# A decoder step with paged caches: cached keys rearranged ahead of the kernel and loaded page by page, and more expert columns folded on VectorE

## The reference

```python
def compressed_branch(q, pos, kv, w1, b1, w2):
    ...
    sub = kv.reshape(bsz, kv.shape[1] // CMP_STRIDE, CMP_STRIDE, 2, A_KV, A_DH)
    first = jnp.einsum('bnlcgd,cldh->bncgh', sub, w1[:, :CMP_STRIDE])
    second = jnp.einsum('bnlcgd,cldh->bncgh', sub, w1[:, CMP_STRIDE:])
    hid = jax.nn.gelu((first[:, :-1] + second[:, 1:]).astype(jnp.float32) + b1.astype(jnp.float32)[:, None, :], approximate=False)
    ckv = jnp.einsum('bncgh,chd->bncgd', hid.astype(kv.dtype), w2)
    ...
```

## Time and profile before

| | |
|---|---|
| median of 3 runs | 2576.49 us (2570.51 to 2578.44) |
| profiled execution, its own time | 2571.7 us |
| its span | 2569.9 us |
| mean granted clock of TensorE | 0.861 of 2.4 GHz |
| busy: TensorE, VectorE, ScalarE, GpSimd | 1970.7, 1468.7, 916.4, 942.9 us |
| moved by DMA | 805.61 MB, mean 313 GB/s |

### The profile page before, as it was taken

The page is one execution under the profiler, slowest core; times in us unless marked ns, Lnnn a source line. Parts: engine busy times, 40 slices in busy tenths (PEclk is TensorE's granted clock), DMA queues, the critical chain, the costliest instruction groups (busy, mean ns, idle before and its releaser), DMA issues. The chain is left out here.

```text
span 2569.9 us, 23064 instructions
## 1 busy us (share of the span) xinstructions
PE 1970.7 (77%) x6950; PEld 981.6 (38%) x6950; DVE 1468.7 (57%) x3134; ACT 916.4 (36%) x2462; POOL 942.9 (37%) x839
## 2 busy tenths in 40 slices
PE   5999797788888777977768688875677777739765
PEld 4436565344444334545212345362122333313211
DVE  1025256895666535774874455758447666664564
ACT  1112103687777323631232234412134444422222
POOL 2021033677554323342653332426233333122551
PEclk9975799899899888998889777987789899969979
DMA  6232518978999989898989986976789888989697
GB/s 194 99 143 74 172 54 334 367 320 345 420 420 420 413 332 388 348 405 302 411 347 387 351 328 229 368 292 270 309 339 358 346 346 347 353 291 359 244 420 296
DMA packets 170226, 805.61 MB, mean 313 GB/s; under 512 B 32564, under 2 KB 37176, under 8 KB 86648
## 3 DMA queue, kind: packets, MB, share of 16 engines
q0 software_dynamic: 93552, 673.78, 66.0%
q1 hardware_dynamic: 76408, 130.37, 14.2%
q10 hardware_dynamic: 144, 0.00, 0.0%
HBM read 798.37 MB, written 14.04 MB: 316 GB/s over the span
## 5 line engine op out<-in xcount | busy, mean ns | idle before, releaser
L3076 POOL DMA_INDIRECT g_uv<-in_peer_uv_dram,f_idx x320 | 389.6, 1217 | 642.0 <-PE g_acc L3193 512.3
L3193 PE MATMUL g_acc<-g_uv,g_diag 128*128 128x512 f32 (+1 forms) x848 | 451.7, 670 | 110.8 <-ACT g_diag L3165 109.1
L3119 DVE CUSTOM_DVE_ANT_0 g_uv<-g_uv,f_h 128x1024 f32<-128x1024 f32 x320 | 405.2, 1271 | 212.1 <-DMA g_uv<-in_peer_uv_dram,f_idx 204.4
L3076 POOL DMA_INDIRECT f_u<-in_peer_uv_dram,f_idx x256 | 299.6, 1170 | 491.9 <-PE g_acc L3193 383.9
L3119 DVE CUSTOM_DVE_ANT_0 f_u<-f_u,f_h 128x1024 f32<-128x1024 f32 x256 | 325.0, 1276 | 180.6 <-DMA f_u<-in_peer_uv_dram,f_idx 174.9
L3193 PE MATMUL g_acc<-f_u,g_diag 128*128 128x512 f32 (+1 forms) x676 | 356.4, 661 | 69.3 <-ACT g_diag L3165 51.7
L3145 ACT ACTIVATE g_gelu<-g_dot 128x2 f32<-128x2 f32 x288 | 58.3, 203 | 763.6 <-DVE g_dot L3119 762.4
L3193 PEld LDWEIGHTS g_acc<-g_uv,g_diag 128*128 128x128 f32 (+1 forms) x848 | 156.9, 197 | 353.3 <-issue 336.4
L3193 PEld LDWEIGHTS g_acc<-f_u,g_diag 128*128 128x128 f32 (+1 forms) x676 | 125.4, 198 | 254.8 <-issue 234.1
L1241 PE MATMUL g_side<-g_slab 128*128 128x512 f32 (+3 forms) x288 | 128.9, 589 | 55.0 <-DMA g_slab<-in_nsa_w_in_dram 52.4
L1101 PE MATMUL g_side<-g_slab 128*128 128x512 f32 x256 | 135.9, 613 | 13.6 <-ACT g_slab L1139 11.9
(11 more groups left out here) (406 smaller groups left out, 2678.8 us busy)
## 6 DMA issues: line engine op xcount, KB each, us to landing
g_slab<-in_nsa_w_in_dram SPq DMA_DIRECT2D x15, 2048.0 KB, 19.1
g_slab<-in_peer_w_q_dram SPq DMA_DIRECT2D x14, 2048.0 KB, 22.2
mp_w<-in_mlstm_w_in_dram SPq DMA_DIRECT2D x6, 2048.0 KB, 10.0
g_slab<-in_nsa_w_out_dram SPq DMA_DIRECT2D x6, 2048.0 KB, 8.4
g_slab<-in_state_win_kv_dram SPq DMA_DIRECT2D x8, 1024.0 KB, 7.7
out_win_s_dram<-in_state_win_kv_dram SPq DMA_DIRECT2D x1, 8128.0 KB
g_uv<-in_peer_uv_dram,f_idx POOLq DMA_INDIRECT x320, 10.8
f_u<-in_mlstm_w_out_dram SPq DMA_DIRECT2D x2, 2048.0 KB, 11.0
```

The source lines that it names most:

```text
L3076: pool.indirect_dma_start(both(i), None, table, bass.IndirectOffsetOnAxis(ap=idx[:, col:col + 1], axis=0), element_offset=layer * PK * PK ...
L3119: dve.tensor_tensor_reduce(row(i, 0), row(i, 0), h[:, t, :], 1.0, 0.0, ALU.mult, ALU.add, dot[:, g % DRING, k:k + 1]).then_inc(dotted, 1)
L3193: mm = pe.matmul(acc[0:n, a, :], diag[:, q % DIAGS, 0:n], row(i, 1)[:, a * 512:a * 512 + 512], start=i == opens[s], stop=i == closes[s])
```

## The change

Before the launch the host writes the caches in another order (`turned`): a page's keys with the key's elements across the 128 partitions, as the products read them, and the values as they were. The window and the compressed MLP's weights are rearranged too. In the kernel the transposes (L1090, L2210) and their copies (L1139, L2349, L2351) are gone, and the products read the loaded rows.

GpSimd's 64 gathers of pages (L1075, L2152) are gone. SyncE loads each page by a number that it reads from the page table into a register (`S.page`): 256 loads of 128 KB for the compressed branch (1 KB to a partition, two buffers of 16 pages, a load waits until the products of the unit two before are done) and 128 of 256 KB for the selected one (2 KB to a partition, waiting for the part three before). The compressed branch now runs in 16 units, keys and values of a sequence apart, of 16 beats from beat 32. The MLP's weights come in 3 loads, three times. `load_stage` keeps only the loads. In `SHARES` 42 more columns are folded on VectorE (237 of 512 in place of 195).

```diff
 class Shared:
+    def page(self, sp, b, k):
+        at = NPAGE * b + k
+        return sp.value_load(self.pages[0:1, at:at + 1], min_val=0, max_val=self.I["sel_turned"].shape[0] - 1)
...
 class CachedBlocks:
-    START = 38
-    UNIT = 2 * CSTR
-    TILES = 4
+    START = 32
+    UNIT = 16
+    UNITS = 2 * DEC_B
...
+    def sync(self, sp):
+        S, I = self.S, self.S.I
+        sp.wait_ge(self.first.projected, 2 * NJ)
+        sp.dma_start(self.w1.rearrange("p c k f h -> p (c k f h)"), I["cmp_w1_rows"]).then_inc(self.weights_in, 16)
+        sp.dma_start(self.w2.rearrange("p c d -> p (c d)"), I["cmp_w2_rows"]).then_inc(self.weights_in, 16)
...
+        for b in range(DEC_B):
+            page = [S.page(sp, b, k) for k in range(NPAGE)]
+            for c in range(2):
+                v = 2 * b + c
+                if v >= 2:
+                    sp.wait_ge(self.multiplied, 8 * (v - 1))
+                for k in range(NPAGE):
+                    sp.dma_start(self.rows[:, v % 2, k, :], I["cmp_turned"][bass.ds(page[k], 1), c].rearrange(
+                        "u p n -> (u p) n")).then_inc(self.rows_in[v % 2], 16)
+
+    def product(self, pe, v, k):
+        b, c = divmod(v, 2)
+        if k == 0:
+            pe.wait_ge(self.rows_in[v % 2], 16 * NPAGE * (v // 2 + 1))
...
+        rhs = self.rows[:, v % 2].rearrange("p a (k g n) -> p k g a n", k=8, g=AG)[:, k]
+        pe.matmul(self.ps_h[c].rearrange("p g (a n) -> p g a n", n=8), self.w1[:, c, k].rearrange("p f h -> p (f h)"), rhs,
+                  start=(k == 0), stop=(k == 7)).then_inc(self.multiplied, 1)
...
 class DecodeWork:
-    def turn(self, pe, p, k):
...
+        pe.matmul(self.bank[1][r0:r0 + 32].rearrange("p (l j) -> p l j", l=4), self.q_blk[:, 2 * PARTS[p][1] + b2, a, :],
+                  self.tiles[:, slot, :, 0, a * P:(a + 1) * P], start=True, stop=True).then_inc(self.multiplied, 1)
...
-    def copy_keys(self, engine, e):
...
+        def load(p):
+            branch, u, q = PARTS[p]
+            if p >= 3:
+                sp.wait_ge(self.summed, p - 2)
+            for b2 in range(2):
+                slot = (2 * p + b2) % SLOTS
...
+                for k in range(4):
+                    page = S.page(sp, 2 * u + b2, 4 * q + k)
+                    sp.dma_start(self.rows[:, slot, 2 * GD * k:2 * GD * (k + 1)], I["sel_turned"][bass.ds(page, 1)].rearrange(
+                        "u p n -> (u p) n")).then_inc(self.landed[slot], 16)
...
+        for p in range(3):
+            load(p)
         for u in range(4):
             sp.wait_ge(self.b_done, u + 1)
             save(0, u, self.o_cmp[:, u, :])
...
+        for p in range(3, len(PARTS)):
+            load(p)
+            if p % 4 == 0 and p >= 8:
+                sp.wait_ge(self.o_ready, p // 4 - 1)
+                save(1, p // 4 - 2, self.o[:, p // 4 - 2, :])
...
-SHARES = ((0, (3,)), (160, (1, 3)), (300, (3,)), (393, (1, 3)), (483, ()), (577, (1, 3)), (772, ()), (836, (3,)),
-          (950, (1, 2, 3)), (1154, ()), (1238, (1, 3)))
+SHARES = ((0, (3,)), (160, (1, 3)), (483, (3,)), (577, (1, 3)), (772, (3,)), (836, (1, 3)), (950, (1, 2, 3)),
+          (1154, (3,)), (1238, (1, 3)))
```

More of the change, by code:

```diff
@@ L1063 @@
[L1063 to L1077, removed]
@@ L1081, in turn @@
[L1081 to L1092, removed]
@@ L1094, in product @@
[L1094 to L1102, removed]
+        self.ps_k = S.bank[0][:, 0:2 * P].rearrange("p (a n) -> p a n", a=2)
@@ L1118, in pe @@
         pe.wait_ge(self.weights_in, 16 * self.LOADS)
-        for b in range(DEC_B + 1):
-            for r in range(0, self.UNIT if b < DEC_B else 8, 2):
-                yield from at(self.START + self.UNIT * b + r)
-                q = CSTR * b + r // 2
-                if b < DEC_B:
-                    self.turn(pe, q)
-                if 1 < q <= CSTR * DEC_B + 1:
-                    self.product(pe, q - 2)
-                if r == 6 and b:
-                    self.outputs(pe, b - 1)
-        self.S.leave(pe, self.out_cp, 2 * DEC_B)
@@ L1142, in split @@
-    def split(self, act, b, c):
-        act.wait_ge(self.multiplied, CSTR * b + (14, 16)[c])
-        if b:
-            act.wait_ge(self.pre_ready, 2 * (b - 1) + c + 1)
-        act.activation(self.second[:, c], self.ps_h[c][ADH:P], ACT.Copy).then_inc(self.second_ready, 1)
-    def squash(self, act, b, c):
-        act.wait_ge(self.pre_ready, 2 * b + c + 1)
-        act.activation(self.hid[:, c, :, 0:N_CMP], self.pre[:, c, :, 0:N_CMP], ACT.Gelu, bias=self.b1[:, c:c + 1]
-                       ).then_inc(self.hid_ready, 1)
+        for v in range(self.UNITS + 1):
+            for k in range(8):
+                yield from at(self.START + self.UNIT * v + 2 * k)
+                if v < self.UNITS:
+                    self.product(pe, v, k)
+                if k == 4 and v and v % 2 == 0:
+                    self.outputs(pe, v // 2 - 1)
+                    if v == self.UNITS:
+                        break
@@ L1189, in dve @@
         self.S.enter(dve, 1)
-        for b in range(DEC_B):
-            for c in range(2):
-                yield from at(self.START + self.UNIT * b + 32 + 4 * c)
-                self.meet(dve, b, c)
+        for v in range(self.UNITS):
+            yield from at(self.START + self.UNIT * (v + 1) + 3)
+            self.meet(dve, v)
 NP_JOBS = [(AQW + br * 2 * GD, WB) for br in range(3)] + [(AQW + AKVW, 3 * AH), (0, WB), (WB, WB)]
@@ L1795, in sync @@
             sp.wait_ge(route.scored, NJ)
[L1796 to L1798 removed]
+        proj.sync(sp, t, rows_used)
+        sp.dma_start(self.w2.rearrange("p c d -> p (c d)"), I["cmp_w2_rows"]).then_inc(self.cw_in, 16)
         with S.nc.allow_non_contiguous_dma(reason="128 biases"):
@@ L2145, in pool @@
     def pool(self, pool, at):
-        cached = self.I["cache_sel_kv"][0].rearrange("a (n l) c g d -> (a n) (l c g d)", l=PTOK)
-        def load(p):
-            _, u, q = PARTS[p]
-            for b2 in range(2):
-                slot = (2 * p + b2) % SLOTS
-                pool.indirect_dma_start(self.rows[:, slot, :], None, cached, bass.IndirectOffsetOnAxis(
-                    ap=self.S.quarter_idx[:, q, 2 * u + b2:2 * u + b2 + 1], axis=0)).then_inc(self.landed[slot], 16)
         yield from at(self.beat)
@@ L2942, in __init__ @@
         self.first = FirstRoute(st, S, self.ranks, self.route.keys_in, u_ring, v_ring, more, acc, w_out_in, d_scores)
-        self.cached = CachedBlocks(st, S, self.first, [more[:, 0], more[:, 1]])
+        self.cached = CachedBlocks(st, S, self.first)
         self.vec = st.sem("side_vec")
@@ L3047, in weave_stage @@
         diag_ready, applied, added = (st.sem(n) for n in ("diag_ready", "applied", "added"))
-        work = SideWork(st, Shared(nc, st, M, I, O, h, idx, gate, quarter_idx, added),
+        work = SideWork(st, Shared(nc, st, M, I, O, h, idx, gate, pages, added),
                         u_ring, v_ring, more, acc, w_out_in)
```

266 lines of the change are left out of this document (96 added, 170 removed).

## The result

The median went from 2571.7 us (20 runs) to 2548.7 (19 runs); the ratio is 0.9909, with a 95% interval of 0.9895 to 0.9924. A twentieth run of the changed kernel, at 3447.1 us, was in the slow state and is left out. That is a gain of 23 us where 58 were forecast. The profiled execution took 2542.0 us (span 2540.2), 6.7 under the median of its kind; that of before, 2571.7, was at its median.

What follows compares the result with a forecast made beforehand. The bound changes by stage, in a ring of late TensorE, slots, gathers and dots; −2 − 23 + 22 − 2 − 5 − 8 − 4 − 8 − 5 − 23 = −58 gives 2513.7 profiled, 2518 us median; range 2465 to 2590.

Steps and rivals of the forecast that it cites:

- 1-KB piece: Cached page loads: DMA time of one 1-KB piece, not in the trace, taken as 0.050 us, bounds 0.044 and 0.068.
- The engines stay busy through this; I cost it at nothing: Cached blocks: TensorE stalls on late page units and GpSimd stops, but page loads keep the DMA engines busy; cost 0.
- the −23 of the cached blocks: Cached blocks, 380 to 640 us: without transposes and copies gathers go earlier, DMA share 0.87 to 0.96; −23 us.
- The second rival: Starvation: pages stay late, TensorE stalls, DMA share stays 0.87 in cached blocks and parts; 2573 us, chance 0.16.
- The folds: 42 more columns on VectorE: a quarter of TensorE's freed time in two stages, a third in another; −4, −8, −5 us.
- the −5 before: First prompt work, 850 to 1025 us: weights in one plain load, 12 more folded columns; share already 0.96, so −5 us.
- the +22: Cached blocks: 32768 pieces of 1 KB replace 4096 of 8 KB, 102 us in place of 80; +22 us, bounds +10 and +59.
- TensorE's transposes: 512 go in the cached blocks (79.2 us of TensorE), 320 in the decode parts (53.3 us); −23 us forecast in each stage.
- The parts: Decode parts: transposes, copies and GpSimd's page-gather waits go; transfers need 303 us, 316 at share 0.96; −23 us, bounds 303 or no gain.
- The weights: MLP's weights in plain loads end TensorE's waits of 13.8 and 16.8 us in prompt work; −5 and −8 us.
- SyncE: Page loads move to SyncE: 0.62 us an issue plus 0.5 a register load, 9 us a part against 15; it fits.
- The load stage: Start of the kernel: the product and five VectorE steps that make row numbers go; −2 us.

Runs made afterwards that it cites:

- half units: Changed kernel with the same 256 loads of 128 KB, but units of 8 pages in four buffers of half the size: 2529.35 us, ratio 0.9833.
- both edits: Changed kernel with the decode parts' products two beats earlier and cached pages in 2-KB pieces, one 256-KB load a page: 2512.0 us, ratio 0.9747.

## Why the prediction was too high, point by point

The direction was right and the time lies in the range, even in the forecast's own (2490 to 2555); the size was not, 23 us for 58. That it lies in the narrower range is luck: the width was there for a dearer 1-KB piece, which came out at the price taken. Two steps failed.

- **"The engines stay busy through this; I cost it at nothing".** The paragraph had the mechanism (one for one, a unit late, TensorE stalls, the ring fills) and then let it go free. The engines do stay busy while TensorE waits (1.04), and run dry just after it (0.52), because nothing has been gathered meanwhile. It cost some 19 us: that is what half units took away with the same transfers (a part of the waits is still there), and then the stage stands at 466.1, 1.6 under before, where the forecast without the stall had 3. In the terms of the sum it is the −23 of the cached blocks that was lost: 23 us of idle engines were to go, 8 went (32.7 to 24.3), and with half units 23 (to 9.3). The second rival had this stage at +20 (no fill, dearer pieces), and it came out at +17.5, so this stage went nearly as that rival had it; but its sign, a DMA share of 0.87 in the first half and in the parts, did not show. The share rose to 0.92 and 0.93. A stall of this kind shows in TensorE's waits, and only part of it in the share of the transfers.
- **The folds, −17 in the three stages and a part of the −5 before.** "How much is on the path lies between nothing and all of it"; it was nothing that can be measured, on the kernel before, on the changed one and on the one with both edits. A quarter was a number without a row, and none of the rows shown of before gives it; the run with the old shares does: a stage in which TensorE's busy time differs by 20 us at the same length is not set by TensorE. What sets 368 to 428 stays open. That columns 224 to 272 and 368 to 428 came out at −4.5 and −7.5, as forecast, is luck: the first is hardly more than what profiles of the same code differ by (162.5 to 168.8 in the nine kernels with the new shares, 167.0 before), and the second came with the rest of the change, as the old shares have it too.

The other steps:

- *The 1-KB piece,* taken at 0.050 us: 32768 of them took 49 ns each on the mean, measured over the packets of the trace. The price was right, and with 101 us for the pages where 80 were reckoned before, so was the +22.
- *TensorE's transposes,* worth 23 in the cached blocks and most of the 23 in the parts, with their copies: put back without these they cost 15.8 and 15.7. Mechanism right, the size two thirds; what the copies were worth is not shown.
- *The parts,* −23 forecast, −16.8 measured, at a share of 0.93 in place of 0.96; this is the next largest miss. The products had kept the beats that the transposes had needed; with these moved the stage reached 314.0, where the forecast had 316.
- *The weights,* −13 forecast, 14 by the run with the old loads (6 to 22).
- *SyncE,* 0.5 us for a register load: 0.27 and 0.15 of register work, 1.0 us a page in all where 1.12 were taken. It fits, as forecast.
- *The load stage,* −2: −1.5.

Columns 180 to 224 took 3.6 us longer, which no step foresaw; over all the runs with the change they took 134.5 to 140.7, so this is hardly more than what profiles differ by.

## What to carry to other kernels

Two DMA queues that were both full took turns by pieces here, so a queue of small pieces beside one of large ones got a small part of the bytes: a buffer filled that way needs its lead reckoned at that rate (37 us for 2 MB in 1-KB pieces), and larger pieces, or smaller buffers that are free earlier, gain time though the bytes stay the same. When an argument says that a stall will come, put a price on it, even if the busy share says that nothing is idle. After an operation is taken out, look for the beats, banks and waits that were laid out for it; and before work is moved off an engine, look whether the stage's length follows that engine at all.

## What was not expected of the hardware

The turn between the two queues was exact over 100 us, 4535 packets for 4535, with pieces of 8 KB against 2 KB. And TensorE's granted clock fell where work was taken from it, from 0.88 to 0.80 in the parts, and rose to 0.87 when the transposes were put back, so part of a saving in busy time is given back at the 1.2 GHz level: the products of the parts (L2142) took 714 ns each in the mean, after 671 before, with the same median (617).
